# Final stage of a mixture-of-experts step: the last two expert steps kept in SBUF, the branch moved ahead of them, and pairs loaded and summed beside step 16

## The reference, cut to what matters

```python
out = jnp.zeros_like(h)
for gi in range(N_GROUPS):
    a = jnp.einsum('btd,edf->btef', h, w_e_gate[gi])
    u = jnp.einsum('btd,edf->btef', h, w_e_up[gi])
    act = jax.nn.silu(a) * u * combine[..., gi, :, None]
    out = out + jnp.einsum('btef,efd->btd', act, w_e_down[gi])
...
x = x + g2 * hier_moe(h, ...)
y = rmsnorm(x, final_norm)
```

## Time and profile before

| | us |
|---|---|
| median of 3 runs (lowest, highest) | 1172.02 (1171.13, 1174.23) |
| the profiled execution | 1171.43 |
| its span, first to last instruction | 1169.7 |
| TensorE busy in the span | 1068.0 |
| VectorE busy | 568.0 |
| ScalarE busy | 252.2 |
| GpSimd busy | 154.9 |

### The profile page before, as it was taken

The page is one execution under the profiler, slowest core; times in us unless marked ns, Lnnn a source line. Parts: engine busy times, 40 slices in busy tenths (PEclk is TensorE's granted clock), DMA queues, the critical chain, the costliest instruction groups (busy, mean ns, idle before and its releaser), DMA issues. The chain is left out here.

```text
span 1169.7 us, 15168 instructions
## 1 busy us (share of the span) xinstructions
PE 1068.0 (91%) x5901; PEld 700.7 (60%) x5901; DVE 568.0 (49%) x1158; ACT 252.2 (22%) x677; POOL 154.9 (13%) x306
## 2 busy tenths in 40 slices
PE   4899998999999999899999999998977998888776
PEld 3355777777777887788667777763543333333222
DVE  3123737467788495475855455453376121110136
ACT  3110010467632132455110000101021011100011
POOL 3000500012414000132110000100002111201101
PEclk9899999999999999899999999999988999998898
DMA  9986643242324434124382423259549999999975
GB/s 332 341 257 187 199 78 75 37 126 70 73 62 72 109 63 92 38 62 139 117 252 73 72 85 104 92 155 271 217 146 367 421 420 415 418 419 419 410 283 172
DMA packets 97430, 226.34 MB, mean 194 GB/s; under 512 B 21486, under 2 KB 40231, under 8 KB 85170
## 3 DMA queue, kind: packets, MB, share of 16 engines
q1 hardware_dynamic: 87718, 203.22, 53.2%
q10 hardware_dynamic: 4516, 12.22, 3.1%
q0 software_dynamic: 5120, 9.88, 2.3%
HBM read 210.60 MB, written 23.08 MB: 200 GB/s over the span
## 5 line engine op out<-in xcount | busy, mean ns | idle before, releaser
L2796 PE MATMUL ps<-w_gate_up,xT 128*64 128x512 f32 x528 | 128.8, 630 | 19.3 <-DMA w_gate_up<-w_e_up 19.3
L2796 PEld LDWEIGHTS ps<-w_gate_up,xT 128*64 128x64 f32 x528 | 40.0, 144 | 106.0 <-issue 78.8
L695 PE MATMUL ps<-hT,w_ring 128*128 128x288 f32 x384 | 96.6, 412 | 3.7 <-PEq L105 3.7
L2952 DVE TENSOR_TENSOR act<-silu_gate,ps 128x256 f32<-128x256 f32 x17 | 7.2, 421 | 181.8 <-ACT silu_gate L2766 181.8
L695 PEld LDWEIGHTS ps<-hT,w_ring 128*128 128x128 f32 x384 | 73.2, 193 | 23.8 <-issue 4.0
L2815 PE MATMUL ps<-w_down,actT 128*64 128x512 f32 x264 | 62.1, 598 | 8.8 <-DVE actT L2956 8.8
L1345 PE MATMUL ps<-hT,w_ring 128*128 128x288 f32 x264 | 67.8, 406 | 0.0
L1630 DVE SCALAR_TENSOR_TENSOR conv_y<-z_staged,convT,conv_y 128x600 f32<-128x600 f32 x72 | 59.7, 842 | 8.4 <-ACT conv_y L1080 6.6
L1345 PEld LDWEIGHTS ps<-hT,w_ring 128*128 128x128 f32 x264 | 49.3, 190 | 13.2 <-issue 0.5
L2815 PEld LDWEIGHTS ps<-w_down,actT 128*64 128x64 f32 x264 | 18.0, 136 | 41.2 <-issue 29.2
L2722 POOL DMA_INDIRECT pair_scratch<-y_block,pairs x16 | 16.1, 1007 | 199.9 <-ACT y_block L2774 199.9
(11 more groups left out here) (580 smaller groups left out, 2007.8 us busy)
## 6 DMA issues: line engine op xcount, KB each, us to landing
w_down<-w_e_down SPq DMA_DIRECT2D x32, 1024.0 KB, 25.1
w_ring<-w_in SPq DMA_DIRECT2D x15, 2048.0 KB, 13.9
w_gate_up<-w_e_gate SPq DMA_DIRECT2D x28, 1024.0 KB
w_gate_up<-w_e_up SPq DMA_DIRECT2D x28, 1024.0 KB
w_ada_slots<-w_ada SPq DMA_DIRECT2D x8, 2048.0 KB, 8.6
w_gate_up<-w_e_gate SPq DMA_DIRECT2D x10, 512.0 KB, 23.4
w_gate_up<-w_e_up SPq DMA_DIRECT2D x10, 512.0 KB, 24.2
w_ada_slots<-w_ada SPq DMA_DIRECT2D x4, 1024.0 KB, 14.8
```

The lines of the kernel that those rows point to most:

```text
L695: last = nc.tensor.matmul(psum[:, bank + hf, 0:HALF], w[:, c, 128 * q:128 * q + 128], x[:, c, HALF * hf:HALF * hf + HALF], start=c == 0, s ...
L2796: last = te.matmul(psum[side(u), s % 2, :], xT[:, s % 2, c, side(u)], gu[s % GU_BUFS][:, u, :, c, :], start=c == 0, stop=c == KC - 1)
```

## The change

Steps 15 and 16 (`KEPT`) now both stay in SBUF; the last scatter is that of step 14. The branch is taken after step 14 (`MAIN`), and both sides of it hold steps 15 and 16. Into the shorter side some of the final stage is woven: TensorE makes step 15's part of tile 0 between the gate-and-up products of step 16 and its transposes, ScalarE weighs tile 0's first rows ahead of copying step 16, VectorE gates step 15's rows ahead of step 16's activation and adds tile 0's pairs behind it. SP waits for steps 0 to 14, branches, loads the gate, waits for the scatters, and loads pairs and `x_again` for all tiles in the order 0, 1, 4, 2, 3 (`FINAL_ORDER`). At the start there is a second zero fill, a second `slot_rows` and a second `rows_of`.

In the final stage no pair goes through TensorE. For each tile ScalarE weighs the first row, VectorE adds the second (`add_pairs`), GpSimd multiplies by the gate (`gate_pairs`), VectorE adds to `x_again` (`on_x2`), TensorE multiplies both `rows_of` with the kept steps (`kept_product`), VectorE adds that from PSUM (`add_kept`; for the new tokens it multiplies by their gate first) and scales (`finish`).

```diff
+KEPT = (FIXED - 2, FIXED - 1)
+MAIN = FIXED - 2
+FINAL_ORDER = (0, 1, 4, 2, 3)
...
-            sp.wait_ge(gmm, hi if lo else hi - 2)
-        all_steps(sp, run)
+            sp.wait_ge(gmm, hi)
+            sp.wait_ge(dmm, hi)
+
+        def further():
+            run(FIXED, STEPS, STEPS)
+            m.final["loads"](sp)
+        run(0, MAIN, FIXED)
+        branch(sp, further, lambda: m.final["loads"](sp))
...
+                for s in KEPT:
+                    c = block_pair(s)
+                    p.indirect_dma_start(out=m.y_dram[:, :], out_offset=bass.IndirectOffsetOnAxis(ap=m.pairs[:, c:c + 1], axis=0),
+                                         in_=m.y_kept[0][:, :], in_offset=None,
+                                         bounds_check=last_pair, oob_is_err=False).then_inc(zeroed, 16)
...
+        run(0, MAIN, FIXED)
+        branch(pool, further, lambda: scattered(MAIN))
```

ScalarE:

```diff
+        def plain():
+            run(MAIN, LAST)
+            silu(LAST)
+            m.final["weigh"](act, 0)
+            keep_y(LAST)
+        keep_rows(1)
+        run(0, MAIN)
+        branch(act, further, plain)
```

TensorE:

```diff
             for s in range(lo, hi):
                 gate_up(s)
+                if s == 0:
+                    rows_of_kept(0)
                 if s == 1:
                     over_tables()
+                rest(s, ahead)
...
+        def plain():
+            run(MAIN, LAST, FIXED)
+            gate_up(LAST)
+            m.final["kept_product"](pe, 0, 0)
+            rest(LAST, FIXED)
```

VectorE, in the expert stage:

```diff
+        def plain():
+            run(MAIN, LAST, FIXED)
+            m.final["gate_kept"](dve, 0)
+            run(LAST, FIXED, FIXED)
+            m.final["add_pairs"](dve, 0)
+        weights()
+        kept_slots(1)
+        x_evacuate(0)
+        kept_slots(0)
```

The pieces of the final stage that the branch calls, and then the final stage of GpSimd, ScalarE and VectorE:

```diff
+    def loads(sp):
+        sp.dma_start(gp[:, :], m.mod_dram[0, 5 * D:].partition_broadcast(128)).then_inc(gpld, 16)
+        sp.wait_ge(m.all_scattered, 1)
+        for f in range(NT):
+            load_y(sp, f)
+            load_x(sp, f)
+            if f == 1:
+                for b in range(NB):
+                    sp.dma_start(gn[NS * b:NS * b + NS], m.mod_dram[1 + b, 5 * D:].partition_broadcast(NS)).then_inc(gnld, 16)
+        sp.dma_start(fn[:, :], ins["final_norm"].partition_broadcast(128)).then_inc(fnld, 16)
+
+    def weigh(act, f):
+        act.wait_ge(yl[f], 16)
+        nc.scalar.activation(first(f), first(f), ACT.Copy, scale=weight(f, 0)).then_inc(weighed, 1)
+
+    def add_pairs(dve, f):
+        dve.wait_ge(weighed, f + 1)
+        nc.vector.scalar_tensor_tensor(first(f), second(f), weight(f, 1), first(f), ALU.mult, ALU.add).then_inc(added, 1)
+
+    def gate_kept(dve, i):
+        dve.wait_ge(gpld, 16)
+        dve.wait_ge(m.yev, KEPT[i] + 1)
+        nc.vector.tensor_tensor(kept_g[i][:, :], m.y_kept[i][:, :], gp[:, :], ALU.mult).then_inc(keptd, 1)
...
+        def gate_pairs(f):
...
+            pool.wait_ge(added, f + 1)
+            p.tensor_tensor(first(f), first(f), g2(f), ALU.mult).then_inc(gated, 1)
...
+        for f in range(NT - 1):
+            gate_pairs(f)
+        root(0)
+        gate_pairs(NT - 1)
+        for f in range(1, NT):
+            root(f)
...
+        for f in range(1, NT):
+            weigh(act, f)
+        for f in range(NT):
+            act.wait_ge(x3, f + 1)
...
+        def on_x2(f):
+            dve.wait_ge(xl[f], 16)
+            dve.wait_ge(gated, f + 1)
+            v.tensor_tensor(x(f), x(f), first(f), ALU.add).then_inc(based, 1)
+
+        def add_kept(f):
+            dve.wait_ge(ysum, f + 1)
+            dve.wait_ge(based, f + 1)
+            part = banks(f)
+            if f == new:
+                v.tensor_tensor(in_two(yg[:, :]), part, in_two(g2(f)), ALU.mult).then_inc(newd, 1)
+                dve.wait_ge(newd, 1)
+                part = in_two(yg[:, :])
+            v.tensor_tensor(in_two(x(f)), in_two(x(f)), part, ALU.add).then_inc(x3, 1)
...
+        add_pairs(dve, 1)
+        on_x2(0)
+        gate_kept(dve, 1)
+        add_pairs(dve, 2)
+        on_x2(1)
+        add_kept(0)
+        add_pairs(dve, 3)
+        on_x2(2)
+        add_kept(1)
+        finish(0)
+        add_pairs(dve, 4)
+        on_x2(3)
+        add_kept(2)
+        finish(1)
+        on_x2(4)
+        add_kept(3)
+        finish(2)
+        add_kept(4)
+        finish(3)
+        finish(4)
```

More of the change, by code:

```diff
@@ L2659, in expert_programs, with branch @@
     side = lambda u: slice(CAP * u, CAP * u + CAP)
-    def all_steps(eng, run, after=lambda hi: None):
-        run(0, FIXED)
+    def branch(eng, further, plain):
         eng.wait_ge(overd, 1)
@@ L2665, in all_steps @@
         with eng.If(n > 0):
-            run(FIXED, STEPS)
-            after(STEPS)
+            further()
             eng.nop()
         with eng.Else():
-            after(FIXED)
+            plain()
             eng.nop()
@@ L2741, in run, with further @@
                     gather(s + 2)
-                if s != LAST:
-                    scatter(s)
+                scatter(s)
         def scattered(hi):
-            pool.wait_ge(zeroed, 16)
-            pool.wait_ge(sct[0], 16 * even(hi - 1))
-            pool.wait_ge(sct[1], 16 * (hi // 2))
-        all_steps(pool, run, scattered)
+            pool.wait_ge(zeroed, 32)
+            for side in range(2):
+                pool.wait_ge(sct[side], 16 * scattered_ahead(hi, side))
+        def further():
+            run(FIXED, STEPS, STEPS)
+            scattered(STEPS)
+        run(0, MAIN, FIXED)
+        branch(pool, further, lambda: scattered(MAIN))
         p.memset(m.fin_ss[:, :], 1.0).then_inc(m.all_scattered, 1)
@@ new lines, in final_programs @@
+    keptd, ysum, newd, x3, fq, fr, fo = (sem(n) for n in ("kept_gated", "kept_summed", "new_gated", "x3_done", "f_sq", "f_rs", "f_out"))
+    rows = [ROWS[t] for t in FINAL_ORDER]
+    new = FINAL_ORDER.index(4)
+    x = lambda f: x2[0:rows[f], f, :]
+    first, second = (lambda f: y[f][0:rows[f], 0, :]), (lambda f: y[f][0:rows[f], 1, :])
+    g2 = lambda f: (gn if f == new else gp)[0:rows[f], :]
+    weight = lambda f, k: m.w[0:rows[f], POS[FINAL_ORDER[f]], k:k + 1]
+    bank = (2, 0, 6, 4, 2)
@@ new lines, in kept_product @@
+    def kept_product(pe, f, i):
+        te = nc.tensor
+        if f != new:
+            pe.wait_ge(keptd, i + 1)
+        elif i == 1:
+            pe.wait_ge(m.yev, FIXED)
+        if i == 0 and f == 3:
+            pe.wait_ge(m.yev, FIXED)
+        if i == 0 and f == 4:
+            pe.wait_ge(x3, 1)
+        src = m.y_kept[i] if f == new else kept_g[i]
+        for hf in range(2):
+            last = te.matmul(banks(f)[:, hf, :], m.rows_of[i][:, tile_cols(FINAL_ORDER[f])], src[:, 512 * hf:512 * hf + 512], start=i == 0, stop=i == 1)
+        if i == 1:
+            last.then_inc(ysum, 1)
@@ L3062, in sync @@
+    m.final = dict(loads=loads, weigh=weigh, add_pairs=add_pairs, gate_kept=gate_kept, kept_product=kept_product)
+    def sync(sp):
+        for f in range(NT):
+            t = FINAL_ORDER[f]
+            sp.wait_ge(fo, f + 1)
             dst = outs["y_prompt"][0, tile_cols(t), :] if t < 4 else outs["y_sample"].rearrange("b s d -> (b s) d")
-            sp.dma_start(dst, out(t)).then_inc(m.y_stored, 16)
+            sp.dma_start(dst, first(f)).then_inc(m.y_stored, 16)
         sp.wait_ge(m.y_stored, 16 * NT)
@@ new lines, in scalar @@
+        for f in range(1, NT):
+            weigh(act, f)
+        for f in range(NT):
+            act.wait_ge(x3, f + 1)
+            if f:
+                act.wait_ge(fq, f)
+            a.activation(sq[0:rows[f], :], x(f), ACT.Square, accum_out=ss[0:rows[f], f:f + 1]).then_inc(fq, 1)
+    def tensor(pe):
+        kept_product(pe, 1, 0)
+        kept_product(pe, 0, 1)
+        kept_product(pe, 1, 1)
+        for f in range(2, NT):
+            kept_product(pe, f, 0)
+            kept_product(pe, f, 1)
```

304 lines of the change are left out of this document (126 added, 178 removed).

## The result

The changed kernel took 1183.14 us (median of 4 runs, 1182.35 to 1185.79) against 1172.69 us (1171.13 to 1174.23, 4 runs) for the kernel before on the same chip: a ratio of 1.0087, with a 95% interval of 1.0069 to 1.0105. It is 10.5 us slower. I had given 4.7 us, with an upper end of 1180.5.

The account below looks back on a forecast made before the run. Bound: the weight stream through the expert stage, then compute, TensorE and VectorE alternating from 1133.6 to 1165.0. All terms 0 except 4.7 us in the tail: 1171.43 + 4.7 = 1176.1, given as 1176.7 for the median; range 1171.0 to 1180.5.

Parts of the forecast that it names:

- The sign: Whole kernel: the change makes it slower, chance 0.66, against 0.28 for the same and 0.06 for faster.
- The stretch behind step 16: Tail after step 16's last product: VectorE's instructions with GpSimd's products in their way end at 1169.7 against 1165.0, 4.7 us later.
- taking turns: Tail: VectorE and GpSimd block each other on instructions with SBUF inputs, costing 5.3 us, less 0.6 gained otherwise.
- four stalls: Tail: VectorE or a root is held up by GpSimd's products four times; three must vanish to count as no change.
- "Cost 0" for the start of the stage: Start of expert stage: second `rows_of` delays steps 0 to 6 by some 3.2 us, but queued weight transfers hide it.
- without that backlog: Start of expert stage: if no older transfers were queued, the second `rows_of` would cost 3.2 us instead of 0.
- Two products of TensorE (0.86) fit the pause of 0.9: Inside step 16, before TensorE transposes the activation: the woven products take 0.86 us and fit the 0.9 us pause.
- All pairs land by about 1136 to 1139 and bound nothing: Around the end of step 16: pairs, issued from 1114.7 instead of 1129.3, all arrive by 1136 to 1139, costing nothing.
- The zero fill at 0: Ahead of the saturated weight stretch, about 884: the second fill costs 0, with 1.05 us kept for the range.
- The branch at 0: TensorE between steps 14 and 15: a delay of 0 to 0.5 us, mostly taken up by step 16's 0.73 wait; counted 0.
- The rival of a late branch: Between steps 14 and 15: code fetch at twice SP's figure, 11.7 us, adds 5.9, giving 1182.6; chance 0.08.

Follow-up runs that it names:

- e1: Changed kernel with GpSimd's multiplication of the pairs by the gate replaced by a one-column memset; 1178.42 us, 1.0044 of the kernel before.
- e2: Changed kernel without the second slot rows and second `rows_of`, both kept steps using step 16's; 1179.48 us, 1.0052 of the kernel before.
- e8: Changed kernel with TensorE's `kept_product(0, 0)` moved from inside step 16 to behind it; 1180.82 us, 1.0077 of the kernel before.
- e14: Changed kernel with tile 4's loads spread over 128 partitions, `g_new` not loaded and tile 4 gated with `g_prompt`; 1181.4 us, one run.
- e3: Changed kernel with two more indirect zero fills, into another scratch, behind the two there; 1182.74 us, 1.0070 of the kernel before.
- e4: Changed kernel with the branch taken out on every engine, only the plain side's code left; 1183.13 us, 1.0084 of the kernel before.
- e13: Changed kernel with tile 4's pairs and `x_again` loaded as 128 rows over 128 partitions, the eight `g_new` loads kept; 1179.9 us, one run.

## Why the prediction was wrong

The sign and the mechanism of the tail held; the cost of everything ahead of it did not. Point by point, by its own steps:

**The stretch behind step 16: right.** From the start of `add_pairs(1)` to the end of `finish(4)` I had worked out 33.8 us (1135.9 to 1169.7), and it took 33.4 (1142.86 to 1176.23). I gave 5.3 us for taking turns; taking the products away gave 4.7 back (e1). The row of a product at 120 us, far from the change, carried this. The form was a little other than worked out: I had expected four stalls, and two instructions were stretched (3.37 and 2.13 us), while the rest came as waits, 1.55 us of it for TensorE. The Trainium skill ("SBUF — State Buffer", section "SBUF: two separate sides") has the same rule, that whichever of the two engines starts first holds the shared ports for its whole instruction, and here the trace agrees: 3.37 us beside GpSimd, 1.22 without.

**"Cost 0" for the start of the stage: wrong, and the step that failed most.** I had argued that a stream of weights with 5 us queued hides a delay of 3.2 us ("leaves no gap in the stream"). The delay was 2.5 us at the end of step 0, and the stream did lose by it: it moved 402 GB/s instead of 419 in 15 us around and behind the end of step 0, and the first weights of step 15 landed 1.1 us later than in e2, which has no second `rows_of`. In the time e2 gave 3.7 us back. The traces account for 1.1 of these in the stream and for 1.6 in step 15's gate-up product, which differs from run to run; the rest is open. That older transfers were still queued at 912 said nothing about what the stream moved in the 10 us ahead of that. The bound of 3.2 "without that backlog" is near the 3.7, but the mechanism behind it, a delay that passes through whole, is not what the stream shows.

**"Two products of TensorE (0.86) fit the pause of 0.9": wrong by a factor of two.** An fp32 product of 128x512 stands in the trace as two matmuls of 0.43, and `kept_product` makes two such: 4 instructions, 1.98 us in the row at 1133.56. The count was in rows that I had (the tail's first group has 8 records for two tiles, 4 for each). It put the transposition back by 0.9 us, step 16 became 0.6 longer, and e8 found 0.7.

**"All pairs land by about 1136 to 1139 and bound nothing": the first half wrong, the second nearly right.** ScalarE could take them from 1134.6 to 1153.1; I had taken 420 GB/s for all of them. VectorE started at 1142.86, where the copy alone would have allowed 1142.2, and e14, with all loads fast, has a tail 0.8 us shorter. So the term is 0.7 to 0.8 us in single executions, not 0.

**The zero fill at 0: right** (e3). **The branch at 0: right in the time** (e4), but not shown for TensorE: it began step 15 1.1 us after its first weights had landed, and I had given it 0 to 0.5. The rival of a late branch gave nearly the measured time, 1182.6, by a delay of 5.9 us; at most these 1.1 us of its mechanism are there. That its number came near is luck.

The sum as measured, on the profiled executions, has three parts. I had 0, 0 and 4.7 for them.

- 2.2 us of scatter.
- 4.1 us up to the end of step 16: 1.5 by which step 15's first weights landed later (1.1 of it goes with the second `rows_of`, 0.4 is open), 1.1 from there to TensorE's start (the branch, probably), 0.9 in step 15's gate-up product, and 0.6 in step 16, from the woven product.
- 4.6 us in the tail.

TensorE's lower clock in the fifth microsecond of step 15's gate-up product makes some 0.5 of the 0.9, by my estimate (half of what it does in a microsecond). One execution each does not show that the change caused it: in e2 and e4 that product took 8.47 and 8.53 us.

The range failed with it. I had kept 3.2 us in the text as the cost without the backlog and then did not let it reach the upper end. With it the range would have gone to 1183.4, just above the measured 1183.14, and would still have had nothing for the woven product.

## What to carry to other kernels

A stage that waits for a stream of transfers does not swallow a delay at its start only because the trace shows that stream saturated later on. Look at what the stream moves right behind the delay, not only whether the engines are busy, and give such a delay its full length as the upper end.

Work that is moved from TensorE to VectorE and GpSimd together cost here what they take in turns, not what each takes alone. Count their instructions with two inputs in SBUF as one queue, and let the others read PSUM: `add_kept(1)`, which reads PSUM, took its usual 1.21 us in the midst of a product of GpSimd.

When transfers are put forward, ask how many partitions each of them fills. And count an fp32 product in the records of the trace, not in calls of the program.

## What the hardware showed that I had not expected

Transfers that fill only some of the partitions slowed down all that ran beside them. With tile 4's loads (64 rows, 768 KB) and the eight of `g_new` (8 rows each, 256 KB) in the queue, the 16 DMA engines were at a busy share of 0.97 to 1.08 with 171 to 299 GB/s in all, for 18 us. In that time 4.3 MB were moved, of which these loads are 1.0; the rest filled all partitions. With tile 4 spread over 128 partitions only the windows around `g_new` were slow (e13: 231 GB/s, then 411), and with `g_new` gone too none was (e14: 391 to 422 while there was enough to move). The kernel before has them too: the window from 1120 to 1123, in which the loads of the earlier trace rows and `g_new` run, has 221 GB/s at a share of 0.82, and the one from 1144 to 1147, with tile 4 in it, 314 at 1.08, against 418 at 1.01 for pairs alone. I had these numbers and did not ask what they meant.

The Trainium skill ("SBUF — State Buffer", section "Door 1: The DMA port swizzle (why `[64,N]` ≈ `[32,N]`)") says that partitions 0 to 63 reach only 8 of the 16 ports, with 196 GB/s measured for a transfer of that shape and 218 at most. Most of the windows of the slow stretches lie at 157 to 233 GB/s, near these figures. What that section does not say, and the 4.3 MB show, is that full-width transfers in the same queue are held back too; which of them waits for which, no run here separates.
